# Expert retrieval of an encoder block: V of three token tiles by one stream of the whole table, with one-hot matrices made on VectorE

## The chip, the cores and the metric

The kernel runs on one core of one Trainium2 chip. The metric is the device time of one execution in microseconds (us). The core has five engines that each run their own list of instructions in order and meet only at semaphores: TensorE (PE, matrix products into PSUM), VectorE (DVE), ScalarE (ACT), GpSimd (POOL) and SyncE (SP). Transfers run on 16 DMA engines that all queues share. POOL issues the gathers (queue q0), SP the plain loads and stores (queue q1).

## What is computed

One layer of a hybrid encoder over 1024 tokens of width 1024, in f32: an input projection, a bidirectional state-space branch, neighbourhood attention, an output projection, and then a product-key retrieval of experts ("PEER"). The change touches the retrieval alone:

```python
def chunk(xc):                                   # 128 tokens
    q = (xc @ w_q).reshape(128, 8, 2, 128)
    s = einsum('thzd,znd->thzn', q, sub_keys)    # scores of 128 keys, twice per head
    s1, i1 = top_k(s[:, :, 0], 16);  s2, i2 = top_k(s[:, :, 1], 16)
    cand = s1[..., :, None] + s2[..., None, :]
    top, pos = top_k(cand, 16)                   # 16 of 256 pairs
    eidx = (i1 * 128 + i2) at pos                # one of 16384 experts
    gate = softmax(top)
    act = gelu(einsum('thkd,td->thk', u[eidx], xc))
    return einsum('thk,thkd->td', gate * act, v[eidx])
```

Each token picks 8 x 16 = 128 experts, and needs their rows of two tables, `peer_u` and `peer_v`, each of 16384 rows of 1024 f32 (4 KB a row, 64 MB a table).

## The kernel before, in words

The 1024 tokens are 8 tiles of 128 (`TT`). The front of the kernel (conditioning, input projection, state-space scan) ends some 920 us after the start. What follows is `stage_tail`, laid out by hand on a line of **slots**: slot `n` is pick `n % 128` of tile `n // 128`, 1024 slots in all, and every engine's program is written slot by slot. Work of the other branches (attention, state-space recurrence, projections, in three passes of two tiles) is spread over slots -128 to 756 as "lane" jobs: PE products into three PSUM banks `ps_l`, each evicted by ACT or DVE.

In slot `n` of the retrieval:

- POOL issues one gather from `peer_u`: for each of 128 tokens (partitions) the row of its pick, 128 rows x 4 KB = 512 KB, into one of `RU` = 6 rooms (`u_rows`). It waits until DVE has used the room (`u_used`, six slots back).
- DVE waits for the gather and forms the 128 dot products with one instruction of 128 x 1024 (line 2637).
- POOL also issues one gather from `peer_v`, 45 slots behind (`FETCH_AT` and one grain): here the 128 partitions hold 32 picks of 4 tokens. It goes into one of `RV` = 12 rooms (`v_rows`) and waits until PE has summed that room's last content (`v_used`). POOL issues V of a slot ahead of U of the same slot.
- Every fourth slot PE sums four gathered V rooms into `acc` (line 2683) with the weights that ACT has put into `spread`.

The picks of a tile are worked out on DVE ("route": top-16 searches) ahead of their slots. A *grain* is 32 picks (two heads); a tile has 4. `turn_index` and `turn_weight` transpose a grain's indices and weights on PE through the bank `ps_turn`, so that V can be gathered token by token. At the end of a tile `finish_sum`, `finish_square` and `finish_norm` add the residual and normalise on DVE, and SP stores the tile.

So before the change every slot from 45 on moves two gathers of 512 KB, 2048 in all, and after slot 1023 only the last 45 of V are left.

## Time and profile before

| | us |
|---|---|
| median of 3 runs | 4027.4 (4024.05 to 4028.98) |
| the profiled execution: its span | 4023.9 |
| of it: start to the first dot of slot 0 | 920.8 |
| slots 0 to 127 (stage A) | 363.6 |
| slots 128 to 383 (stage B) | 820.6 |
| slots 384 to 639 (stage C) | 781.9 |
| slots 640 to 767 (stage D) | 402.4 |
| slots 768 to 1023 (stage E) | 664.6 |
| after the last dot (stage F) | 70.0 |

The bounds of the stages are the starts of the dot of slots 0, 128, 384, 640 and 768 and the end of the last. The profile is one execution as the hardware recorded it; its own time is the span. A row of the table of waits names who waited, on which line, for whom, then the total, the number of times and the longest.
### The profile page before, as it was taken

The page shows a single profiled execution, that of the slowest core. Times are in us where ns is not written, and L with a number is a line of the kernel's source. Part 1 is how long each engine was busy: PE and PEld are TensorE (multiplying, and loading weights), DVE is VectorE, ACT ScalarE, POOL GpSimd, SP SyncE. Part 2 cuts the span into 40 slices and gives each one's busy share as a digit, 9 for nine tenths or more (in the row PEclk, how much of TensorE's full clock was granted, in tenths as well). Part 3 has the DMA queues.
Part 4 walks back from the last instruction along what each step waited for, and adds up shares of the span by engine and source line. Part 5 has one row for each costly group of instructions (what it writes and reads, how often), then busy time and mean ns, then how long its engine had stood idle before and what let it go on. Part 6 is the DMA issues. An engine that isn't in the chain of part 4 may idle for free.

```text
span 4023.9 us, 41489 instructions
## 1 busy us (share of the span) xinstructions
PE 2788.8 (69%) x14155; PEld 1429.4 (36%) x14155; DVE 2439.3 (61%) x5186; ACT 858.2 (21%) x2057; POOL 2121.6 (53%) x2149
## 2 busy tenths in 40 slices
PE   6899999898975677796676767455757753333334
PEld 4787777544342322333333323122323320000000
DVE  4552446527676666556766665677766667666652
ACT  4333213402143301112333011132320110000000
POOL 1000205013576656556766565676665667777775
PEclk9999999999987888897887888778888875565566
DMA  8944865567999999999999999999999999999998
GB/s 223 258 154 143 228 209 169 180 240 268 413 407 393 403 410 412 413 412 393 393 400 405 412 400 413 401 406 397 392 406 411 389 409 409 410 408 408 402 409 336
DMA packets 472416, 1422.97 MB, mean 354 GB/s; under 512 B 66152, under 2 KB 136784, under 8 KB 464016
## 3 DMA queue, kind: packets, MB, share of 16 engines
q0 software_dynamic: 298768, 1086.75, 69.5%
q1 hardware_dynamic: 173152, 332.95, 23.2%
q8 instruction: 115, 1.88, 0.2%
q10 hardware_dynamic: 288, 0.62, 0.1%
q14 instruction: 93, 0.76, 0.0%
HBM read 1359.46 MB, written 90.06 MB: 360 GB/s over the span
## 4 chain that ended last, share of the span: by engine, by line
DMA 38%; POOL 13%; PE 9%; issue 8%; DVE 8%; ACT 0%; SPq 0%; DVEq 0%; ACTq 0%; POOLq 0%
DMA ring<-in_peer_u,idx 34%; POOL ring L2459 6%; POOL ring L2452 6%; PE ps_l L1775 5%; DMA ring<-in_peer_v,idxT 4%; DVE ring L2637 4%; PE acc L2683 2%; PE ps_l L1853 1%; PE ps_l L1831 0%; DMA lane<-state_scr 0%; DVE e_f L2560 0%; PE ps_l L1848 0%; DVE hit L2558 0%; DVE where L2520 0%; DVE rest L2521 0%
## 5 line engine op out<-in xcount | busy, mean ns | idle before, releaser
L2637 DVE CUSTOM_DVE_ANT_0 ring<-ring,ps_n2F 128x1024 f32<-128x1024 f32 x1024 | 1242.2, 1220 | 933.3 <-DMA ring<-in_peer_u,idx 922.2
L2459 POOL DMA_INDIRECT ring<-in_peer_u,idx x1024 | 999.1, 976 | 805.8 <-DVE dots L2637 576.3
L2683 PE MATMUL acc<-ring,spread 128*32 128x512 f32 x4096 | 734.7, 853 | 953.3 <-DMA ring<-in_peer_v,idxT 953.1
L2452 POOL DMA_INDIRECT ring<-in_peer_v,idxT x1024 | 993.0, 970 | 336.5 <-issue 297.5
L1775 PE MATMUL ps_l<-lane 128*128 128x512 f32 x1760 | 790.2, 603 | 11.6 <-ACT lane L2100 6.6
L2683 PEld LDWEIGHTS acc<-ring,spread 128*32 128x32 f32 x4096 | 147.7, 136 | 1417.6 <-issue 1415.7
L1775 PEld LDWEIGHTS ps_l<-lane 128*128 128x128 f32 x1760 | 330.8, 193 | 443.8 <-issue 431.4
L562 POOL DMA_DIRECT2D bias<-rpb_scr x16 | 13.2, 829 | 322.5 <-PE ps_dt L846 277.0
L1970 PE MATMUL ps_l<-lane 128*128 128x512 f32 x192 | 117.3, 696 | 56.1 <-DVE nmax L2152 55.8
L2489 ACT ACTIVATE dots<-dots 128x32 f32<-128x32 f32 x32 | 7.3, 229 | 606.1 <-DVE dots L2637 605.9
L2060 ACT ACTIVATE st<-st,nmax 128x512 f32<-128x512 f32 x128 | 92.2, 720 | 184.0 <-DVE nmax L2152 182.9
L846 PE MATMUL ps_x<-n_hi,w_x_hi 128*128 128x512 f32 x256 | 103.9, 406 | 13.1 <-DVE w_x_lo L681 13.1
L846 PE MATMUL ps_x<-n_hi,w_qk_hi 128*128 128x512 f32 x256 | 103.2, 403 | 6.6 <-DVE w_qk_lo L757 6.6
L688 DVE TENSOR_TENSOR w_z_lo<-w_z,w_z_hi 128x512 fp32r<-128x512 f32 x64 | 40.7, 688 | 109.1 <-ACT w_z_hi L588 75.1
L1996 PEld LDWEIGHTS ps_l<-lane 128*64 128x64 f32 (+1 forms) x1664 | 66.2, 146 | 108.0 <-ACT lane L2040 56.5
L846 PE MATMUL ps_x<-n_lo,w_x_hi 128*128 128x512 f32 x256 | 102.3, 399 | 0.0
L846 PE MATMUL ps_x<-n_hi,w_x_lo 128*128 128x512 f32 x256 | 102.1, 399 | 0.0
L846 PE MATMUL ps_x<-n_lo,w_qk_hi 128*128 128x512 f32 x256 | 101.9, 398 | 0.0
L846 PE MATMUL ps_x<-n_hi,w_qk_lo 128*128 128x512 f32 x256 | 101.8, 397 | 0.0
L1996 PE MATMUL ps_l<-lane 128*64 128x64 f32 (+1 forms) x1664 | 84.4, 241 | 23.2 <-ACT lane L2040 22.9
L2018 PE MATMUL ps_l<-ident,st 128*128 128x128 f32 x448 | 73.9, 289 | 31.5 <-ACT lane L2049 31.1
L2266 POOL TENSOR_TENSOR ring<-lane,ring 128x4096 f32<-128x4096 f32 x2 | 17.7, 8832 | 139.7 <-DMA lane<-in_w_out 139.7
(363 smaller groups left out, 4014.7 us busy)
## 6 DMA issues: line engine op xcount, KB each, us to landing
lane<-kept_scr SPq DMA_DIRECT2D x44, 2048.0 KB, 10.6
w_z<-in_w_in SPq DMA_DIRECT2D x16, 1024.0 KB, 6.0
adaB<-in_w_ada SPq DMA_DIRECT2D x16, 1024.0 KB, 6.2
ring<-in_peer_u,idx POOLq DMA_INDIRECT x1024
ring<-in_peer_v,idxT POOLq DMA_INDIRECT x1024, 13.8
kept_scr<-in_w_in SPq DMA_DIRECT2D x6, 2048.0 KB
lane<-w_scr SPq DMA_DIRECT2D x6, 2048.0 KB, 10.9
ada<-in_w_ada SPq DMA_DIRECT2D x8, 1024.0 KB, 15.4
```

The costliest lines, as they stand in the source:

```text
L688: nc.vector.tensor_tensor(z_parts[1][q % PLACES][:, :], w_z[:, k // KH, k % KH, :], z_parts[0][q % PLACES][:, :], ALU.subtract).then_inc(z ...
L846: last = nc.tensor.matmul(bank, stationary(left, k), moving(right, k), start=(k == 0 and n == 0), stop=(k == KD - 1 and n == 2))
L1775: last = nc.tensor.matmul(bank, inT[:, f % SETS, k, :], spare_half(c, k // 4)[:, k % 4, :] if weights is None else weights[:, k, :], start ...
L1853: last = nc.tensor.matmul(ps_y[:, h * HEADDIM:(h + 1) * HEADDIM], M4[:, d, h, :], x_dt[:, i, d, hc], start=False, stop=(d == 1 and h == HP ...
L1970: nc.tensor.matmul(scores_bank(a_pass, u), qd[:, p % RP, i, :], kT[:, p % RP, k0:k0 + HALF], start=True, stop=True).then_inc(qk_done, 1)
L1996: last = nc.tensor.matmul(values_bank(a_pass, u)[side(hh), :], PT[keys, u % 2, b, side(hh)], V[keys, p % RP, tile, side(hh)], start=(j == ...
L2018: last = nc.tensor.transpose(turned[:, b * P:(b + 1) * P], probs[:, u % RS, c0:c0 + P], ident[:, :])
L2060: nc.scalar.activation(row[:, GRID_W:], row[:, GRID_W:], ACT.Exp, bias=least, scale=-1.0, accum_out=rsum[:, u % 4:u % 4 + 1]).then_inc(exp ...
L2452: pool.indirect_dma_start(v_rows[:, nv % RV, :], None, a["peer_v"][0], bass.IndirectOffsetOnAxis(ap=idxT[:, m % 2, col:col + 1], axis=0)). ...
L2459: pool.indirect_dma_start(u_rows[:, n % RU, :], None, a["peer_u"][0], bass.IndirectOffsetOnAxis(ap=idx[:, i % RI, j:j + 1], axis=0)).then_ ...
L2637: nc.vector.tensor_tensor_reduce(out=u_rows[:, n % RU, :], in0=u_rows[:, n % RU, :], in1=ps_n[:, :], scale=1.0, scalar=0.0, op0=ALU.mult, ...
L2683: last = nc.tensor.matmul(acc[q * QUAD:(q + 1) * QUAD, cols], spread[:, m % 2, c0:c0 + QUAD], v_rows[:, nv % RV, cols], start=(g == 0 and ...
```

## The change

V of tiles 2, 3 and 4 (`DENSE`) is no longer gathered. Instead:

- **Weight matrices.** For each of the 384 tokens of these tiles a matrix of 128 x 128 is made, whose entry (b, a) is the sum of the weights of the picks with first key a and second key b. DVE makes two one-hot matrices per token with one `tensor_scalar` each (`both_hot`; the second also multiplies by the weight), PE multiplies them (`make_parts`, 4 tokens in one PSUM bank, `ps_turn`), ACT evicts the bank into `parts`, and after 16 tokens ACT itself issues a store of 1 MB into a new DRAM tensor `share_scr`, in pieces of 512 bytes. The room `parts` is single: before it writes the first four tokens of the next 16, ACT waits for that store (`s_stored`). The four rooms of one-hot matrices are single too: DVE waits for the product that read the room four tokens earlier (`part_mm`). `make_parts` stands every third slot (a slot or two later where `ps_turn` is needed otherwise) from slot 9 of the tile that follows, ACT's eviction one slot later.
- **One stream of the table.** From slot 770 to 1046 the whole table `peer_v` is loaded once, in 32 blocks of 512 rows (2 MB) by SP, and the weight matrices are loaded again (48 loads of 0.5 MB). PE multiplies them for the three tiles at once: 192 units of 4 products of 128 x 512 (`multiply_block`) into the three banks `ps_l`, which the lane jobs have left by then. DVE adds each unit to its sum in SBUF two slots later (`add_block`). The three tiles are normalised and stored at the end (`whole_sum` and what follows it).
- **Pace of the gathers.** V of tiles 0 and 1 is spread out: its 256 gathers are issued over 640 slots (two in five slots) from slot 45. Tiles 5 to 7 keep one a slot, 45 slots behind, from slot 685.
- **Rooms.** V has 10 rooms in place of 12, and only 7 until row 340 of V (slot 769), since the other three hold `parts` and the one-hot matrices until the last store. `h` has a room of its own in the ring, and indices and weights are kept for 4 tiles.

All dot products with U, the routes and the lane jobs stay in their slots.

```diff
+DENSE = (2, 3, 4)
+KEYS_TOGETHER = 4
+SHARES = NKEYS // KEYS_TOGETHER
+PART_KEYS, PART_TOKENS = 8, 16
...
+    share_scr = [scratch(f"share_scr_t{t}", [NKEYS // PART_KEYS, NKEYS, P // PART_TOKENS, PART_KEYS * PART_TOKENS]) for t in DENSE]
...
-    RU, RV, RI = 6, 12, 2
+    RU, RV, RI, RH = 6, 10, 2, 4
+    RING = 18
...
-        v_rows = ring[:, RU * DM:].rearrange("p (r d) -> p r d", d=DM)
+        v_rows = ring[:, RU * DM:(RU + RV) * DM].rearrange("p (r d) -> p r d", d=DM)
+        h = ring[:, (RU + RV) * DM:(RU + RV + 1) * DM]
+        kept_row = ring[:, (RU + RV + 1) * DM:(RU + RV + 2) * DM]
+        parts = v_rows[:, RV - 2:RV, :].rearrange("p r d -> p (r d)")
+        pick_row = v_rows[:, RV - 3, :].rearrange("p (s n) -> p s n", n=P)
+        pickT, hot_a = pick_row[:, 0:3, :], pick_row[:, 4:4 + TURNS, :]
+        hot_b = kept_row[:, RH * PICKS:RH * PICKS + TURNS * P].rearrange("p (s n) -> p s n", n=P)
+        weight = kept_row[:, 0:RH * PICKS].rearrange("p (r n) -> p r n", r=RH)
...
+        order = {t: i for i, t in enumerate(SUMMED)}
+        v_grain = [GRAINS * t + g for t in SUMMED for g in range(GRAINS)]
+        pace = GRAINS * (DENSE[-1] + 1) / (GRAINS * len(BEFORE))
+
+        def fetch_slot(s, k):
+
+            m = v_grain[s]
+            if m < GRAINS * DENSE[0]:
+                return FETCH_AT + int(pace * (s * GRAIN + k))
+            return m * GRAIN + FETCH_AT + k
...
+        ALL_ROWS_FROM = PICKS * len(BEFORE) + 84
+        v_row = [nv % (RV - 3) if nv < ALL_ROWS_FROM else (nv - ALL_ROWS_FROM) % RV for nv in range(len(SUMMED) * PICKS)]
...
+            n += PART_AT - PICK_TURN_AT
+            for k in range(P // TURNS):
+                while turning & {n, n + 1}:
+                    n += 1
+                part_mm_at[n], part_ev_at[n + 1] = i * P // TURNS + k, i * P // TURNS + k
+                for r, before in enumerate((2, 2, 1, 1)):
+                    hot_at.setdefault(n - before, []).append(i * P + k * TURNS + r)
+                n += PART_STEP
...
+        DENSE_FROM, DENSE_TO, DENSE_LAG = PICKS * 6 + 2, PICKS * TT + 22, 2
...
+        unit_slot = [DENSE_FROM + q * (DENSE_TO - DENSE_FROM) // ALL_BLOCK_UNITS for q in range(ALL_BLOCK_UNITS)]
+        unit_at, added_at, block_at = {}, {}, {}
+        for q, n in enumerate(unit_slot):
+            unit_at.setdefault(n, []).append(q)
+            added_at.setdefault(n + DENSE_LAG, []).append(q)
...
+        v_blocks = a["peer_v"][0].rearrange("(c i b) d -> c b i d", i=KEYS_TOGETHER, b=NKEYS)
...
+        def load_shares(sp, c):
+
+            if c == 0:
+                sp.wait_ge(p_mm, LANE_JOBS)
+                sp.wait_ge(p_norm, TT)
+                for r in range(MIX):
+                    sp.wait_ge(s_keep[r], 16 * TT // MIX)
+            if c >= 2:
+                sp.wait_ge(block_mm, (c - 1) * UNITS_A_SHARE)
+            sp.dma_start(v_block[:, c % 2, :, :], v_blocks[c]).then_inc(s_block[c % 2], 16)
+            s, first = divmod(c * KEYS_TOGETHER, PART_KEYS)
+            if first == 0:
+                if s == 0:
+                    sp.wait_ge(s_stored, 16 * ND * P // PART_TOKENS)
+                for i in range(ND):
+                    sp.dma_start(shares[s % 2][i], share_scr[i][s].rearrange("b g n -> b (g n)")).then_inc(s_part[s % 2], 16)
+
...
+                            if v_before[nv] is not None:
+                                pool.wait_ge(v_used, v_before[nv] // QUADS + 1)
+                            elif nv >= ALL_ROWS_FROM:
+                                pool.wait_ge(s_stored, 16 * ND * P // PART_TOKENS)
...
+                        if n in part_ev_at:
+                            k = part_ev_at[n]
+                            group, turn = divmod(k * TURNS, PART_TOKENS)
+                            act.wait_ge(part_mm, (k + 1) * TURNS)
+                            if k and turn == 0:
+                                act.wait_ge(s_stored, 16 * group)
+                            nc.scalar.activation(parts.rearrange("p (c t e) -> p t c e", t=PART_TOKENS, e=PART_KEYS)[:, turn:turn + TURNS, :, :],
+                                                 ps_turn[:, :].rearrange("p (t c e) -> p t c e", t=TURNS, e=PART_KEYS), ACT.Copy).then_inc(part_ev, 1)
+                            if turn == PART_TOKENS - TURNS:
+                                act.wait_ge(part_ev, k + 1)
+                                d, g = divmod(group, P // PART_TOKENS)
+                                nc.scalar.dma_start(share_scr[d][:, :, g, :].rearrange("c b n -> b c n"),
+                                                    parts.rearrange("p (c n) -> p c n", n=PART_KEYS * PART_TOKENS)).then_inc(s_stored, 16)
...
+                def both_hot(u):
+
+                    if u >= TURNS:
+                        v.wait_ge(part_mm, u - TURNS + 1)
+                    k = u % P
+                    nc.vector.tensor_scalar(hot_a[:, u % TURNS, :], every_key[:, :], pickT[:, 0, k:k + 1], None, ALU.is_equal).then_inc(hot_a_done, 1)
+                    nc.vector.tensor_scalar(hot_b[:, u % TURNS, :], every_key[:, :], pickT[:, 1, k:k + 1], pickT[:, 2, k:k + 1], ALU.is_equal, ALU.mult).then_inc(hot_b_done, 1)
...
+                def add_block(q):
+
+                    c, i, half = block_unit(q)
+                    total = whole[i][:, half * HALF:(half + 1) * HALF]
+                    bank = ps_l[:, q % LANE_BANKS * HALF:(q % LANE_BANKS + 1) * HALF]
+                    if q == 0:
+                        v.wait_ge(p_mm, LANE_JOBS)
+                        v.wait_ge(p_act, LANE_ACTS)
+                        for k in range(len(st_jobs))[-RS:]:
+                            stored_wait(v, k)
+                    v.wait_ge(block_mm, q + 1)
+                    if c == 0:
+                        nc.vector.tensor_copy(total, bank).then_inc(block_added, 1)
+                    else:
+                        v.wait_ge(block_added, q - UNITS_A_SHARE + 1)
+                        nc.vector.tensor_tensor(total, total, bank, ALU.add).then_inc(block_added, 1)
...
+                def turned_bank_read(kind, number):
+
+                    if turned_last[0] is not None:
+                        was, i = turned_last[0]
+                        if was == "index":
+                            pe.wait_ge(idxT_done, i + 1)
+                        elif was == "weight":
+                            pe.wait_ge(spread_done, TOGETHER * (i + 1))
+                        elif was == "picks":
+                            pe.wait_ge(picks_split, i + 1)
+                        else:
+                            pe.wait_ge(part_ev, i + 1)
+                    turned_last[0] = kind, number
...
+                def make_parts(k):
+
+                    pe.wait_ge(hot_a_done, (k + 1) * TURNS)
+                    pe.wait_ge(hot_b_done, (k + 1) * TURNS)
+                    turned_bank_read("parts", k)
+                    for r in range(TURNS):
+                        nc.tensor.matmul(ps_turn[:, r * P:(r + 1) * P], hot_b[:, r, :], hot_a[:, r, :], start=True, stop=True).then_inc(part_mm, 1)
...
+                def multiply_block(q):
+
+                    c, i, half = block_unit(q)
+                    bank = ps_l[:, q % LANE_BANKS * HALF:(q % LANE_BANKS + 1) * HALF]
+                    if q == 0:
+                        pe.wait_ge(p_act, LANE_ACTS)
+                        pe.wait_ge(p_dve, LANE_DVES)
+                    if q % UNITS_A_SHARE == 0:
+                        pe.wait_ge(s_block[c % 2], 16 * (c // 2 + 1))
+                        s = c * KEYS_TOGETHER // PART_KEYS
+                        pe.wait_ge(s_part[s % 2], 16 * ND * (s // 2 + 1))
+                    if q >= LANE_BANKS:
+                        pe.wait_ge(block_added, q - LANE_BANKS + 1)
+                    s, first = divmod(c * KEYS_TOGETHER, PART_KEYS)
+                    share = shares[s % 2][i].rearrange("p (n e) -> p e n", e=PART_KEYS)
+                    for k in range(KEYS_TOGETHER):
+                        last = nc.tensor.matmul(bank, share[:, first + k, :], v_block[:, c % 2, k, half * HALF:(half + 1) * HALF],
+                                                start=(k == 0), stop=(k == KEYS_TOGETHER - 1))
+                    last.then_inc(block_mm, 1)
```

## Rows read from the trace of the kernel before

**Rows 1.** The page: span, busy times of the engines, DMA share in 40 slices.

```profile
span 4023.9 us, 41489 instructions
...
PE 2788.8 (69%) x14155; PEld 1429.4 (36%) x14155; DVE 2439.3 (61%) x5186; ACT 858.2 (21%) x2057; POOL 2121.6 (53%) x2149
...
DMA  8944865567999999999999999999999999999998
```

**Rows 2.** Windows of stages A to F: PE, PEld, DVE, ACT, POOL busy (instructions), clock, DMA, GB/s.

```profile
920.80:1284.40 363.60, 285.75 (x1252) 139.76 (x1254) 256.42 (x584) 104.61 (x278) 218.83 (x220) 0.88 0.98 382
1284.40:2105.00 820.60, 601.42 (x3256) 270.87 (x3252) 524.53 (x1216) 201.06 (x541) 506.07 (x514) 0.87 1.02 404
2105.00:2886.90 781.90, 513.34 (x2800) 223.26 (x2792) 519.94 (x1192) 173.02 (x474) 498.34 (x513) 0.81 1.02 404
2886.90:3289.30 402.40, 285.25 (x1483) 120.36 (x1486) 256.28 (x591) 71.70 (x182) 244.75 (x256) 0.84 1.01 402
3289.30:3953.90 664.60, 232.77 (x1148) 50.30 (x1140) 437.85 (x968) 39.32 (x95) 486.37 (x510) 0.56 1.03 408
3953.90:4023.90 70.00, 36.88 (x200) 7.74 (x200) 6.98 (x12) 2.57 (x7) 34.01 (x36) 0.65 0.78 305
```

**Rows 3.** Waits of DVE, the longest of stages A to E in order: us, times, longest.

```profile
DVE ring L2637 <- DMA ring<-in_peer_u,idx: 75.4, 44, 5.2
...
DVE ring L2637 <- DMA ring<-in_peer_u,idx: 260.7, 160, 7.9
...
DVE ring L2637 <- DMA ring<-in_peer_u,idx: 236.6, 155, 6.3
...
DVE ring L2637 <- DMA ring<-in_peer_u,idx: 132.5, 78, 9.0
...
DVE ring L2637 <- DMA ring<-in_peer_u,idx: 217.1, 176, 3.5
```

**Rows 4.** DMA view of stage E: gathers issued, median us to landing.

```profile
ring<-in_peer_v,idxT POOLq DMA_INDIRECT x259, 13.3
ring<-in_peer_u,idx POOLq DMA_INDIRECT x251
```

**Rows 5.** DMA view of 46 to 58 us, stores of 512-byte pieces: packets, MB, share.

```profile
q1 hardware_dynamic: 3988, 2.00, 58.1%
...
n_scr<-BT SPq DMA_DIRECT2D x6, 384.0 KB, 2.8
```

**Rows 6.** Lines 724, 2193 and 2213 on DVE: ns min/median/max, start, form.

```profile
L724 DVE TENSOR_SCALAR conv<-padded,taps x16: 750/754/755, 68.1 to 271.4; 128x1024 f32<-128x1024 f32 x16
...
L2193 DVE TENSOR_SCALAR lstat<-lstat x8: 153/154/155, 874.4 to 3144.7; 128x1 f32<-128x1 f32 x8
...
L2213 DVE TENSOR_TENSOR lane<-lane,ps_l x14: 681/685/689, 884.7 to 3142.7; 128x512 f32<-128x512 f32 x14
```

**Rows 7.** Groups of DVE before 920 us, one row: count, busy us, mean ns.

```profile
L1061 DVE TENSOR_TENSOR cb<-ps_cb,upto 128x128 f32<-128x128 f32 x8 | 2.3, 285 | 0.7 <-PE ps_cb L1123 0.7
```

**Rows 8.** Groups of ACT from 920 us on, one row: busy us, mean ns.

```profile
L2123 ACT ACTIVATE lane<-ps_l 128x512 f32<-128x512 f32 x12 | 7.2, 597 | 45.3 <-PE ps_l L1775 45.3
```

**Rows 9.** DMA view of 1332.3 to 1338.0 us: packets, MB, share, by queue.

```profile
DMA packets 1073, 2.10 MB, mean 368 GB/s; under 512 B 593, under 2 KB 593, under 8 KB 1073
...
q0 software_dynamic: 537, 1.97, 94.0%
q1 hardware_dynamic: 536, 0.13, 11.4%
```

**Rows 10.** Line 2452, gathers of V: us from issue to landing.

```profile
DMA to landing us min/median/max: 7.0/13.8/25.3
```

**Rows 11.** Window of line 1775 alone: PE busy, PEld busy, clock, DMA, GB/s.

```profile
980.55:1018.51 37.96, 37.96 (x88) 16.57 (x88) 1.00 0.85 322
```

**Rows 12.** Window of line 2683 alone, stage E: same columns.

```profile
3289.30:3953.90 664.60, 231.05 (x1020) 43.23 (x1012) 0.56 1.03 408
```

**Rows 13.** Waits of POOL, stage E, one row: us, times, longest.

```profile
POOL ring L2452 <- PE acc L2683: 4.4, 10, 1.7
```

More of the change, by code:

```diff
@@ L1187, in stage_tail @@
     LANE_BANKS = 3
+    TURNS = 4
     ctx = ExitStack()
@@ new lines, in stage_tail @@
+        for c in range(SHARES):
+            block_at.setdefault(unit_slot[(c - 1) * UNITS_A_SHARE] + 1 if c >= 2 else DENSE_FROM - 6 + c, []).append(c)
+        WHOLE_SUM = DENSE_TO + DENSE_LAG + 2
+        RESIDUAL_SLOT, WHOLE_ROOT, WHOLE_NORM = PICKS * (TT - 1) + 8, WHOLE_SUM + 3 * ND + 1, WHOLE_SUM + 3 * ND + 4
+        LANE_JOBS = len(evac_of)
+        LANE_ACTS, LANE_DVES = acts, dves
+        DROOM = KEYS_TOGETHER * DM
+        v_block = lane[:, 0:2 * DROOM].rearrange("p (r a d) -> p r a d", r=2, a=KEYS_TOGETHER)
```

284 lines of the change are left out of this document (191 added, 93 removed).

## The prediction, made before the change was run

> **What bounds the kernel now.** I read the page first, then the windows by stage, then who waits for whom. On the page the DMA digits stand at 9 from slice 11 on, while PE, DVE and POOL are busy 53 to 69% [rows 1]. The windows say the same stage by stage: the DMA share is 0.98 in A and 1.01 to 1.03 in B to E (packets overlap a little, so about 1.02 is full), and no engine fills its stage [rows 2]. The waits of DVE confirm it: its one long wait in each stage is for the gather of U [rows 3]. So from slot 0 on, 3103 of 4024 us, the 16 DMA engines bound the kernel. In E almost nothing but gathers moves: 259 + 251 gathers in 664.6 us [rows 2, 4], so one gather of 512 KB costs **1.30 us** of all DMA engines. That is the price for the rest of this text.
>
> The second limit is DVE. Stage time less its wait for U is the time that DVE needs for everything else [rows 2, 3]: A 288, B 560, C 545, D 270, E 448 us. It will matter once transfers are taken away.
>
> **The change, part by part.** In total it takes away 384 gathers of V (499 us at 1.30) and adds the table (32 loads of 2 MB, as much as 128 gathers: 166 us), the loads of the weight matrices (48 of 0.5 MB: 62 us) and 24 stores of 2048 pieces of 512 bytes. For these the row of the 512-byte stores gives 3988 packets in 58.1% of 12 us, 1.75 ns of all engines each [rows 5], so 3.6 us a store and 86 us in all. On the DMA engines alone the balance is 499 - 166 - 62 - 86 = **185 us** to the good. But it is uneven: what is removed lies in slots 45 to 685, what is added lies in slots 770 to 1046, where DMA is full already. So I go by stages.
>
> A (363.6): V falls from 83 to 33 rooms, -50 x 1.30 = -65, to 299; but V starts at slot 45 and the first half runs behind the last projection jobs of PE, which gain nothing. Middle between 299 and 363.6: **331**.
>
> B (820.6): V falls from 256 to 102, -154 x 1.30 = -200. DMA then needs 620, DVE 560. Neither is even over the stage, so now one and now the other will be last, and I take 4% on top: **645**.
>
> C (781.9): the same -200, and 16 of the 24 stores, +57: DMA needs 639. DVE gets 256 tokens x 2 one-hot instructions of 128 x 128. Their price: `tensor_scalar` took 754 ns for 1024 elements a partition and 154 for one [rows 6], on a straight line 229 for 128; bounds are 154 and the 285 of a two-operand instruction of 128 x 128 [rows 7]. I take 225, nearest to the same kind of instruction: 512 x 0.225 = 115 us (79 to 146). DVE then needs 545 + 115 = 660 (624 to 691) and is the bound. ACT's evictions at about 0.6 us [rows 8], 64 here, go beside an ACT that is busy 173 of 782 [rows 2], and PE's small products beside a PE that gives up three fifths of its V sums; both cost nothing while their queue is not held up.
>
> The waits added here are the open point. ACT waits for the store three slots after it issued it; behind that wait stand gelu, the spreading of weights and the evictions of the lane. PE's next `make_parts` but one needs ACT's eviction, and DVE's one-hot instructions stand behind that product, six slots after the store was issued; at 2.7 us a slot DVE has 16 us in hand. What does a store take? Alone 2.8 us for 768 pieces [rows 5]. Beside gathers, small packets and gather packets go through one for one: in a stretch of 5.7 us there are 537 packets of q0 and 536 of q1, 256 bytes for the most part [rows 9]. 2048 pieces at that pace need 4 x 5.7 + 2.8 = 25.6 us while the gather queue is never empty. With DVE as the bound that queue is empty part of the time (DMA work 639 of 660), and V's rows are few, so the store lands sooner; I allow 2.5 us a store, between 0 and 9.2: 16 x 2.5 = 40. **700**.
>
> The Trainium skill ("DMA: Bandwidth & Descriptors", § Queues, rings and completion order) says that a DMA engine takes turns between its queues by whole packets, typically 9 to 17 descriptors. The trace agrees on turns, but shows them at the grain of single pieces. By the page a store's 128 pieces an engine would be 8 to 14 turns, each against at most one gather's share (8 pieces of 0.165, by 1.30 x 16 / 128): 14 to 22 us a store; the allowance of 40 us would nearly vanish and the sum be about 3952.
>
> D (402.4): V falls from 128 to 45 x 0.4 + 83 = 101, -35; 8 stores +29: DMA needs 396, DVE 270 + 58 = 328. From slot 685 to 769 V goes at one a slot with 7 rooms. Then the last row of a batch of four reuses a room of the batch just ahead, so four slots must hold one trip from issue over landing (7.0 to 25.3, median 13.8 [rows 10]) to the sum: 4 x 3.3 = 13 us against that median. It fits only because POOL's pause thins the queue that makes the landing long; I allow 15 us (0 to 60). **411**.
>
> E (664.6): 92% of the stream lies here, (166 + 62) x 0.92 = +210: DMA needs 875. DVE adds 177 units at 0.685 [rows 6], 448 + 121 = 569, covered. POOL still has its two gathers a slot, 486 busy us [rows 2], covered. PE gets 707 products of 128 x 128 x 512, two records each, at 38.0/88 = 0.431 us a record at full clock [rows 11]: 609 us, beside 231 us of V sums at clock 0.56 [rows 12], 130 at full clock: 739 us of full-clock work in 875. In B a busy PE was granted 0.87 [rows 2]: 849. So PE is nearly as late as DMA. V has 10 rooms, so a room must come back within seven slots, 24 us, against a landing of 13.3 now [rows 4] plus the queue of the stream; POOL waited 4.4 us for V's rooms here so far [rows 13]. I allow 15 us: **890**.
>
> F (70.0): 8% of the stream, +18, and 3 for the closing of three more tiles, which lies ahead of the last sum: **91**.
>
> Sum: 331 + 645 + 700 + 411 + 890 + 91 = 3068 in place of 3103, -35 us. The profiled span of 4024 stands 3.4 us below the median, so the forecast is 4027.4 - 35, about **3992 us**: most of the 185 us of DMA time is given back in C (DVE) and by stages that are no longer evenly filled.
>
> **Rivals.** (1) *The store holds ACT, and ACT holds all* (slower). If the gather queue stays full, each store takes 25.6 us and DVE loses 25.6 - 16.4 = 9.2 us at each of 16 stores in C; in D a slot is 3.3 us, six are 20, so 5.6 us at each of 8. 147 + 45 = 192 in place of 40, about 4140 us. It decides from a landing of some 16 us on. For it speaks the row of packets one for one [rows 9]; against it, that a waiting DVE stops the gathers, which empties the queue and speeds the store. (2) *PE bounds the stream* (slower). If PE, held by every V row in turn, is granted 0.75 rather than 0.87, E takes 739/0.75 = 985, +95: about 4087. It decides below 0.84, where PE passes DMA's 875. For it: clock 0.56 in E now; against it: 0.81 to 0.88 wherever PE had lane work [rows 2]. (3) *All stages run at the larger of their two limits*: A 320, B 625, C 660, D 396, E 875, F 88, together 2964, about 3888. For it: POOL is busy in E for 486 of 665 us beside a full DMA and costs nothing [rows 2]; two near limits need not add up. Against: the room rules above.
>
> **How the numbers follow.** Chances: my forecast (3950 to 4040) 0.42, rival 3 (or most of it) 0.21, rival 1 0.22, rival 2 0.15. Within 0.2% is +-8 us, about what a measurement of this kernel can tell from no change. The forecast case is faster with 0.28, the same with 0.08, slower with 0.06; rival 3 is faster; rivals 1 and 2 are slower but for 0.02. Faster 0.49, same 0.10, slower 0.41. Cases of both signs hold much, so the range goes from 3895 to 4130: it leaves out the better half of rival 3's end and the worse half of rival 1's. The likeliest case's own range is 3950 to 4040.
>
> **What would show it.** In the profile after: DMA work by stage and DVE's wait for U. If B falls by about 175 us, the price per gather is right. If C falls by about 80 with DVE's wait for U near zero, DVE is its bound; if C doesn't fall and DVE waits for PE at the one-hot lines and ACT for the store's landing, it is rival 1. If E is over 940 with PE busy over 90% and DMA share under 0.97, it is rival 2. POOL's wait for PE's V sums in D gives the price of the seven rooms. The prediction is wrong if one-hot instructions take near 0.4 us, or if the stream is not hidden behind PE at all.

## The result, and the profile after

| | before | after | predicted |
|---|---|---|---|
| median | 4028.09 us (4 runs) | 4153.28 us (4 runs, 4150.12 to 4163.51) | 3992 (3895 to 4130) |
| after / before | | 1.0321, 95% interval 1.0307 to 1.0336 | 0.991 |
| A, slots 0 to 127 | 363.6 | 337.5 | 331 |
| B, 128 to 383 | 820.6 | 662.0 | 645 |
| C, 384 to 639 | 781.9 | **788.5** | 700 |
| D, 640 to 767 | 402.4 | **452.0** | 411 |
| E, 768 to 1023 | 664.6 | 888.9 | 890 |
| F, after the last dot | 70.0 | 109.3 | 91 |

The change made the kernel 3.2% slower, and the prediction had the sign wrong. The stages are those of one profiled execution, the slowest of the four (span 4161.3, as a run 4163.5). They add up to 3238 in place of the forecast 3068: 170 us too many, of which C has 88, D 41 and F 18.

The page of after, its span, busy times and DMA share in 40 slices (answers to [rows 1]):

```profile
span 4161.3 us, 43453 instructions
...
PE 3294.9 (79%) x14737; PEld 1971.8 (47%) x14737; DVE 2713.7 (65%) x6146; ACT 894.5 (21%) x2099; POOL 1758.0 (42%) x1766
...
DMA  8945865568999999999887987999899999999996
```

Before, the DMA digits are 9 from slice 11 to the last but one. Now there are holes between slices 20 and 30, which lie in C and D. The windows of stages A to F (columns as in [rows 2]) say how large they are:

```profile
923.10:1260.60 337.50, 259.83 (x1028) 133.76 (x1026) 254.74 (x581) 103.70 (x273) 167.57 (x167) 0.88 0.92 339
1260.60:1922.60 662.00, 521.76 (x2560) 257.46 (x2560) 512.68 (x1204) 193.02 (x519) 355.10 (x359) 0.88 0.98 376
1922.60:2711.10 788.50, 504.97 (x2615) 291.74 (x2616) 617.44 (x1695) 200.58 (x513) 356.45 (x359) 0.79 0.87 314
2711.10:3163.10 452.00, 307.10 (x1622) 154.53 (x1624) 314.05 (x852) 89.01 (x210) 214.68 (x223) 0.83 0.92 349
3163.10:4052.00 888.90, 782.54 (x2564) 473.51 (x2556) 545.89 (x1146) 39.14 (x96) 492.84 (x517) 0.95 1.02 408
4052.00:4161.34 109.34, 84.17 (x320) 43.82 (x320) 32.19 (x44) 2.79 (x8) 36.88 (x38) 0.86 0.64 233
```

C has 0.87 x 788.5 = 686 us of DMA work and 617 us of DVE work, and takes 788: neither fills it. So the reader asks who waits there. The waits of DVE, ACT and PE in C, the longest of each (who waited, for whom, total us, times, longest):

```profile
DVE ring L2746 <- PE ps_turn L2918: 94.1, 19, 21.5
DVE idxT L2802 <- PE ps_turn L2868: 21.0, 2, 20.0
DVE ring L2822 <- DMA ring<-in_peer_u,idx: 12.6, 6, 3.3
...
ACT ring L2612 <- PE ps_turn L2918: 197.2, 46, 11.4
ACT ring L2612 <- DMA share_scr_t<-ring: 191.8, 12, 33.0
...
PE ps_turn L2918 <- DVE ring L2747: 70.9, 13, 8.8
PE ps_turn L2918 <- ACT ring L2612: 60.9, 6, 18.5
PE ps_turn L2868 <- ACT ring L2612: 25.0, 2, 24.2
```

Line 2822 is the dot (2637 before), 2746 and 2747 the one-hot instructions, 2918 the product of weight matrices, 2612 ACT's eviction of it. DVE's wait for U, 236.6 us before [rows 3], is 12.6: DMA no longer bounds C. In its place stands a chain: ACT waits 192 us for stores to land, PE waits 61 and 25 us for ACT, DVE 94 us for PE.

The queue that ACT's stores use and their landing, DMA view of C (packets, MB, share; then issues, KB, median us to landing):

```profile
q10 hardware_dynamic: 33024, 16.78, 7.2%
...
share_scr_t<-ring ACTq DMA_DIRECT2D x16, 1024.0 KB, 18.0
```

7.2% of 788.5 is 57 us of all DMA engines, just what the prediction charged for them. The 18.0 us to landing are the trouble, as the first experiment shows. One store shows how. The timeline of ACT, PE and DVE around it (start, us, engine, line, operation; in brackets the idle time before and what ended it):

```profile
2199.69 0.60 ACT L2612 ACTIVATE ring<-ps_turn 128x512 f32<-128x512 f32 x1 [9.35 <-PE ps_turn L2918]
2200.32 0.37 ACTq L2617 DMA_DIRECT2D share_scr_t<-ring  x1
2217.55 0.60 ACT L2612 ACTIVATE ring<-ps_turn 128x512 f32<-128x512 f32 x1 [17.26 <-DMA share_scr_t<-ring]
2218.04 1.08 ACT L2116 ACTIVATE lane<-ps_l 128x512 f32<-128x512 f32 x2
...
2219.27 3.75 PE L1791 MATMUL ps_l<-lane 128*128 128x512 f32 x4 [9.71 <-ACT lane L2116]
2222.81 1.44 PE L2918 MATMUL ps_turn<-ring 128*128 128x128 f32 x8
...
2213.89 1.22 DVE L2822 CUSTOM_DVE_ANT_0 ring<-ring,ps_n2F 128x1024 f32<-128x1024 f32 x1
2215.03 0.08 DVE L2822 DVE_READ_ACCUMULATOR2_ANT dots<- 128x1 f32 x1
2223.48 0.29 DVE L2746 TENSOR_SCALAR ring<-every_key,ring 128x128 f32<-128x128 f32 x1 [8.37 <-PE ps_turn L2918]
```

The store goes out at 2200.3 and lands 17.1 us later. DVE runs on until 2215.1 and then stands 8.4 us. Of these only 2.4 lie before the landing (in most of the long waits more does, see below): after it ACT evicts the bank, then a lane bank (line 2116), PE makes the lane product that waited for that (3.75 us), and only then the product that DVE waits for.

In D and E the same table has, for POOL and ACT in D, DVE in E, and DVE in F:

```profile
POOL ring L2570 <- PE acc L2900: 126.6, 20, 23.4
...
ACT ring L2612 <- DMA share_scr_t<-ring: 105.0, 6, 26.2
...
DVE ring L2822 <- DMA ring<-in_peer_u,idx: 313.5, 180, 12.1
...
DVE st L2764 <- PE ps_l L2936: 38.3, 9, 7.5
```

### The profile page after: what moved, and what is told of

It reads as the page before. It is cut to its first block and busy times, and to the rows that moved or that the text cites. A ratio compares the mean times of both kernels' runs of the same rounds, so it can differ in the third digit from the quotient of the medians.

```text
span 4161.3 us, 43453 instructions
## 1 busy us (share of the span) xinstructions
PE 3294.9 (79%) x14737; PEld 1971.8 (47%) x14737; DVE 2713.7 (65%) x6146; ACT 894.5 (21%) x2099; POOL 1758.0 (42%) x1766
## 5 line engine op out<-in xcount | busy, mean ns | idle before, releaser
L1791 PE MATMUL ps_l<-lane 128*128 128x512 f32 x1760 | 799.7, 609 | 65.0 <-ACT st L2121 27.2
L2570 POOL DMA_INDIRECT ring<-in_peer_v,idxT x640 | 622.0, 972 | 424.8 <-PE acc L2900 245.8
L2936 PE MATMUL ps_l<-lane 128*128 128x512 f32 x1280 | 583.5, 610 | 6.0 <-DMA lane<-share_scr_t 6.0
L1791 PEld LDWEIGHTS ps_l<-lane 128*128 128x128 f32 x1760 | 334.9, 195 | 488.5 <-issue 449.6
L2900 PE MATMUL acc<-ring,spread 128*32 128x512 f32 x2560 | 380.7, 721 | 232.4 <-DMA ring<-in_peer_v,idxT 232.2
L2936 PEld LDWEIGHTS ps_l<-lane 128*128 128x128 f32 x1280 | 396.4, 315 | 199.5 <-issue 63.1
L2918 PE MATMUL ps_turn<-ring 128*128 128x128 f32 x768 | 134.4, 331 | 174.5 <-DVE ring L2747 70.9
L2918 PEld LDWEIGHTS ps_turn<-ring 128*128 128x128 f32 x768 | 123.3, 238 | 216.8 <-DVE ring L2746 123.0
L2746 DVE TENSOR_SCALAR ring<-every_key,ring 128x128 f32<-128x128 f32 x384 | 112.0, 292 | 114.0 <-PE ps_turn L2918 113.9
L1986 PE MATMUL ps_l<-lane 128*128 128x512 f32 x192 | 128.7, 760 | 45.7 <-DVE columns L2168 45.7
L2747 DVE TENSOR_SCALAR ring<-every_key,ring 128x128 f32<-128x128 f32 x384 | 133.7, 348 | 0.0
L2076 ACT ACTIVATE st<-st,columns 128x512 f32<-128x512 f32 x128 | 92.1, 720 | 147.5 <-DVE columns L2168 146.3
L2764 DVE TENSOR_TENSOR st<-st,ps_l 128x512 f32<-128x512 f32 x124 | 84.7, 684 | 52.5 <-PE ps_l L2936 52.5
L2936 PE MATMUL ps_l<-lane,gin 128*128 128x512 f32 x256 | 116.7, 606 | 0.0
## 6 DMA issues: line engine op xcount, KB each, us to landing
share_scr_t<-ring ACTq DMA_DIRECT2D x24, 1024.0 KB, 18.4
```

The source lines that it names most:

```text
L1791: last = nc.tensor.matmul(bank, inT[:, f % SETS, k, :], spare_half(c, k // 4)[:, k % 4, :] if weights is None else weights[:, k, :], start ...
L1986: nc.tensor.matmul(scores_bank(a_pass, u), qd[:, p % RP, i, :], kT[:, p % RP, k0:k0 + HALF], start=True, stop=True).then_inc(qk_done, 1)
L2076: nc.scalar.activation(row[:, GRID_W:], row[:, GRID_W:], ACT.Exp, bias=least, scale=-1.0, accum_out=rsum[:, u % 4:u % 4 + 1]).then_inc(exp ...
L2570: pool.indirect_dma_start(v_rows[:, v_row[nv], :], None, a["peer_v"][0], bass.IndirectOffsetOnAxis(ap=idxT[:, m % 2, col:col + 1], axis=0) ...
L2746: nc.vector.tensor_scalar(hot_a[:, u % TURNS, :], every_key[:, :], pickT[:, 0, k:k + 1], None, ALU.is_equal).then_inc(hot_a_done, 1)
L2747: nc.vector.tensor_scalar(hot_b[:, u % TURNS, :], every_key[:, :], pickT[:, 1, k:k + 1], pickT[:, 2, k:k + 1], ALU.is_equal, ALU.mult).the ...
```

## The experiments

Line numbers move by a few between these kernels. Stages are given as in the table; in every run A lies between 334 and 342 and B between 652 and 665, so only C to F are told; E ends here, and in the column before, at the start of the last dot and in the column after at its end, 1.2 us later. All runs but two were timed once, with the kernel before at a median of 4021.5 to 4028.4 us beside them. Four executions of the changed kernel lie 13 us apart, and the B of all runs, which these edits hardly touch, 12: a step of 10 us in a stage shows nothing. Theories of the first runs: the store's landing (S) and the price of the one-hot instructions (H).

### Stores in 128 pieces of 8 KB

```diff
...
-nc.scalar.dma_start(share_scr[d][:, :, g, :].rearrange("c b n -> b c n"),
-                    parts.rearrange("p (c n) -> p c n", n=PART_KEYS * PART_TOKENS)).then_inc(s_stored, 16)
+nc.scalar.dma_start(share_scr[d][g], parts).then_inc(s_stored, 16)
```

> The store of 16 tokens goes out as 128 pieces of 8 KB in place of 2048 of 512 bytes (same bytes, other order in DRAM, and the loads of the stream keep their 4 KB pieces, so tiles 2 to 4 get weight matrices in the wrong order). Theory S (ACT's wait for the store holds PE and DVE): the landing falls from a median of 18.4 us to some 8, ACT's wait for it in stage C from 192 us to under 30, C from 788 to about 700 and D from 452 to about 420; the whole about 4035. Rival H (the one-hot instructions are too dear: 282 + 342 ns a token in place of 450) and rival L (DVE, PE and ACT wait for one another at every four tokens, store or not): C falls by at most 25, the whole stays over 4120.

Measured: 4060.8 us (before on the same chip 4023.8); C 712.0, D 429.1, E 880.3, F 109.3. The DMA view of this run over the whole kernel, where the changed kernel has 18.4 in the last column, and ACT's wait for the store in C:

```profile
share_scr_t<-ring ACTq DMA_DIRECT2D x24, 1024.0 KB, 8.1
```

```profile
ACT ring L2612 <- DMA share_scr_t<-ring: 69.8, 8, 12.1
```

The same bytes, in a sixteenth of the pieces, land in 8.1 us instead of 18.4, ACT waits 70 us instead of 192, DVE 34 for the products instead of 94, and C and D give back 76 and 23 us. The whole run is 93 us faster than the changed kernel's median, which is 125 us slower than before.

### One-hot matrices for one token in four

```diff
 if u >= TURNS:
+    if u % TURNS:
+        return
     v.wait_ge(part_mm, u - TURNS + 1)
...
-pe.wait_ge(hot_a_done, (k + 1) * TURNS)
-pe.wait_ge(hot_b_done, (k + 1) * TURNS)
+pe.wait_ge(hot_a_done, TURNS + k)
+pe.wait_ge(hot_b_done, TURNS + k)
```

> DVE makes the two one-hot matrices for one token of four only; the products of the other three read those of the first four tokens (weights of tiles 2 to 4 are wrong). All waits, products, evictions and stores stay. It takes 288 x 0.62 = 179 us of work from DVE, 119 of it in stage C and 60 in D. Theory H: C falls by 100 or more to under 690, D by 40, the whole to about 4010. Theory S: the waits for the store stay and eat most of it: C falls by under 50, the whole stays over 4090.

Measured: 4137.5; C 766.5, D 448.4. DVE's busy time in C falls from 617 to 532 us, the stage by 22. Of the 85 us that DVE is spared, 33 come back as waits at the next one-hot line (127 for 94) and some 30 as waits elsewhere. The waits of ACT and DVE in C:

```profile
ACT ring L2612 <- DMA share_scr_t<-ring: 209.0, 11, 26.2
...
DVE ring L2748 <- PE ps_turn L2920: 127.2, 23, 22.3
```

With the small pieces in place it is the store that sets the pace, and H alone is not the cause.

### No weight matrices at all, with 7 and with 10 rooms

```diff
-sp.dma_start(shares[s % 2][i], share_scr[i][s].rearrange("b g n -> b (g n)")).then_inc(s_part[s % 2], 16)
+sp.dma_start(shares[s % 2][i], a["peer_u"][0, (s * ND + i) * P:(s * ND + i + 1) * P, :]).then_inc(s_part[s % 2], 16)
...
-if n in part_ev_at:
+if False:
...
-    split_picks(split_at[n])
-    both_hot(u)
-    turn_picks(pick_turn_at[n])
-    make_parts(part_mm_at[n])
```

> No weight matrices are made at all (no one-hot matrices, products, evictions, stores); the stream loads rows of the U table in their place, as many bytes in the same pieces. Tiles 2 to 4 come out wrong. Pace of the gathers, rooms and stream stay. It measures what the making of the matrices costs in all: by the sum of the prediction without stores and one-hot work C is 581 by DMA and 545 by DVE, so about 605; D 367 by DMA, about 385 if seven rooms cost little (theory R, seven rooms of V bound D from slot 685 on: D stays over 410). The whole about 3930 to 3960.

and with that

```diff
-ALL_ROWS_FROM = PICKS * len(BEFORE) + 84
+ALL_ROWS_FROM = 0
```

> As the kernel without weight matrices, and all ten rooms of V in use from the first row on. Theory R (seven rooms bound D): D falls by 25 us or more against that kernel and POOL's wait for the V sums in D from some 100 us to under 20. Rival: D moves by under 8 us, the rooms were not what D waited for.

Measured: 3915.9, C 605.2, D 398.2, E 879.0, F 110.8; with ten rooms of V from the start 3891.5, C 604.2, D 384.0, E 873.5. So making and storing the matrices costs 183 us in C and 54 in D, and the seven rooms cost 14 in D, between the two expectations. C is a DMA-bound stage again here, with share 0.99:

```profile
1920.60:2525.80 605.20, 402.36 (x2099) 201.17 (x2100) 500.33 (x1173) 163.81 (x450) 354.92 (x359) 0.82 0.99 382
```

Were the matrices free, the stream would bring 2.7 to 3.3%.

### Both first edits at once

> Store as 128 pieces of 8 KB and one-hot matrices of one token in four only: both edits of the first two runs at once, so the weight matrices are wrong. It asks what is left of stage C (712 us with the whole store, 605 without any weight matrices). Theory W (what is left is the price of 512 one-hot instructions on an engine that is then the bound): three quarters of them are 0.75 x 256 x 0.453 = 87 us, C 625 to 640, D about 400, total 3960 to 3985. Rival L (the chain DVE, PE, ACT and back over the single rooms holds DVE whatever the instructions take): C over 690, D over 420, total 4040 to 4060.

Measured: 4007.8; C 681.6, D 416.9. Between the two ranges that were expected: 30 us for three quarters of the one-hot instructions (87 by their price). DMA share in C is 0.95 here, so the next limit stands close behind.

### Small pieces at the load instead of the store

The store as in the first experiment, and

```diff
-sp.dma_start(shares[s % 2][i], share_scr[i][s].rearrange("b g n -> b (g n)")).then_inc(s_part[s % 2], 16)
+sp.dma_start(shares[s % 2][i].rearrange("p (g n) -> p g n", n=PART_KEYS * PART_TOKENS),
+             share_scr[i][:, :, s * PART_KEYS * PART_TOKENS:(s + 1) * PART_KEYS * PART_TOKENS].rearrange("g b n -> b g n")).then_inc(s_part[s % 2], 16)
```

> The store goes out in 128 pieces of 8 KB and the stream loads the weight matrices in 512-byte pieces instead (48 loads of 1024 pieces): the same result, with the small pieces moved from where ACT waits for them to where SP's queue is two blocks ahead. Theory S (what hurts is that the store's landing is waited for, not that its pieces cost DMA time): C 712 and D 429 as with the whole store; E gains 86 - 62 = 24 us of DMA work and stands at 905 to 915; total 4080 to 4100. Rival D (the small pieces cost the same wherever they stand): the 92 us come back in E, 970 or more, total 4150.

Measured: 4229.3; C 719.1, D 419.5, E 1062.0. C and D are near those of the whole store, but E is 182 us above that run, far over the 24 of theory S; it is over 970, as rival D has it, but the growth is twice the 92 us that rival D has come back. PE's longest wait in E, and the loads of the weight matrices in the DMA view of E (18.1 us to landing in the run with whole stores):

```profile
PE ps_l L2936 <- issue: 269.4, 14, 22.9
```

```profile
lane<-share_scr_t SPq DMA_DIRECT2D x37, 512.0 KB, 32.7
```

PE stands 14 times, about 19 us each, with 16 sets of loads in all: the wait seems to have moved with the pieces. The trace names no releaser for it; the next edit tells, which issues each load one block of the stream earlier:

```diff
...
-s, first = divmod(c * KEYS_TOGETHER, PART_KEYS)
-if first == 0:
+s = 0 if c == 0 else (c + 1) // 2
+if c % 2 == 1 and c + 1 < SHARES or c == 0:
```

> As the run with the small pieces at the load (stage E 1062 us there, PE waiting 14 times some 19 us for weight matrices that took 31.5 us to land), but each load of weight matrices is issued one block of the stream earlier, some 27 us. Theory S (small pieces cost by being waited for, and 24 us of DMA work otherwise): E 900 to 920, total 4070 to 4100. Rival D (pieces of 512 bytes slow everything beside them): E over 980, total over 4150.

Measured: 4068.6; C 713.5, D 423.0, E 904.0. The same loads take a median of 36.5 us to land, PE waits 1.7 us for them, and the 269 us are gone. E is 23.7 us above the whole-store run, the 24 of DMA work that the price of 1.75 ns a piece gives. So small pieces have two prices: a small one on the engines, and a large one for whoever waits for them.

### More slots between a store and the wait for it

```diff
+base = n
 for k in range(P // TURNS):
+    if k % (PART_TOKENS // TURNS) == 0:
+        n = base + k // (PART_TOKENS // TURNS) * 14
...
-    for r, before in enumerate((2, 2, 1, 1)):
+    for r, before in enumerate((1, 1, 0, 0)):
...
-    n += PART_STEP
+    n += 2
```

> The products of 16 tokens stand two slots apart and then a gap follows (14 slots a group as before), so that ACT's next wait for the store comes some 9 slots after its issue in place of 3 and DVE's some 11 in place of 6; everything else as in the changed kernel. Theory S: a store that lands in 18 us (33 at most) is then over before anyone asks: ACT's waits for the store in C fall from 192 us to under 40, C to 705 to 725, D to 425 to 440, total 4055 to 4085. Rival T (the small pieces themselves delay the gathers, and the wait is only where it shows): C stays at 770 to 790, total 4140 to 4155.

Measured: 4142.6; C 746.0, D 472.1. Neither expectation: C gains 42 us, D loses 20. ACT still waits 107 us in C, 6 times:

```profile
ACT ring L2615 <- DMA share_scr_t<-ring: 107.2, 6, 29.0
```

Two of these stores, issued at 2018.3 and 2065.9, kept ACT until 33.0 and 36.5 us later, where the longest landing in the changed kernel was 32.9. A likely reason, which no run here isolates, is that gathers go on while nobody is held, so that a store with its 2048 pieces lands later: 15 gathers were issued in those 33.0 us, and 8 in the 29.0 us that the same store took in the changed kernel. What D loses was not taken apart further.

### The stream ends earlier

```diff
-DENSE_FROM, DENSE_TO, DENSE_LAG = PICKS * 6 + 2, PICKS * TT + 22, 2
+DENSE_FROM, DENSE_TO, DENSE_LAG = PICKS * 6 + 2, PICKS * TT - 4, 2
```

> The stream's units are spread over slots 770 to 1020 instead of 770 to 1046, everything else as in the changed kernel. It asks what sets stage F (109 us). Theory P (PE works off the units of the last 22 slots after the last dot, 15 units of 8 records at 0.43 us, 52 us): F falls to 55 to 70, E grows by 8% of the PE work if PE is its bound (to about 940) or by less than 20 us if DMA is; total 4110 to 4150. Rival Q (F is the chain of sums, normalising and storing the three tiles and not the stream): F stays above 95.

Measured: 4137.5; E 898.8, F 77.2. Windows of E and F, and DVE's longest wait in F:

```profile
3159.30:4058.10 898.80, 829.72 (x2696) 511.12 (x2692) 554.85 (x1159) 39.10 (x95) 491.63 (x514) 0.97 1.02 405
4058.10:4135.28 77.18, 36.42 (x192) 7.47 (x184) 21.87 (x31) 2.79 (x8) 41.48 (x42) 0.65 0.82 313
```

```profile
DVE acc L2781 <- PE acc L2900: 51.3, 1, 51.3
```

P holds, if less than in full (55 to 70 were expected): without the stream's last units PE has 36 us of work in F instead of 84, and F ends with the last sum of V, as before the change (70.0). E pays some 10 of the 32 us.

### A better version, and half the one-hot work on ACT

Whole stores, small pieces at the load, issued early, the stream's earlier end, and

```diff
+base = n
 for k in range(P // TURNS):
+    if k % (PART_TOKENS // TURNS) == 0:
+        n = max(n, base + k // (PART_TOKENS // TURNS) * 14)
...
```

> As the run before it, and each group of 16 tokens begins 14 slots after the last at the soonest (products three slots apart as before), so that ACT's next wait for a store comes some 5 slots after its issue, and the units of the stream end at slot 1020. Theory S with theory P for stage F: a whole store lands in 8 us (14 at most) and is over before ACT asks for it; C falls from 719 to between 655 (DVE's own 617 and its waits for U and lanes) and 685, D to 400 to 420, F to 75 to 80; total 3990 to 4040. Rival L (the chain DVE, PE, ACT over the single rooms sets C without any wait for a store): C stays at 700 to 720, total 4045 to 4080.

Measured: 4050.9, 1.0068 times before (95% interval 1.0051 to 1.0085); C 704.2, D 421.7, E 918.7, F 76.6. ACT waits 19 us for stores in C, in place of 192, and still C is 704: rival L's figure, not S's. This is the fastest kernel found that computes the same outputs; it is still slower than the kernel before.

The same kernel with the first one-hot matrix made on ACT:

```diff
...
+one = hot_a[:, u % TURNS, :]
+nc.scalar.activation(one, every_key[:, :], ACT.Abs, bias=pickT[:, 0, u % P:u % P + 1], scale=-1.0).then_inc(hot_x, 1)
+act.wait_ge(hot_x, u + 1)
+nc.scalar.activation(one, one, ACT.Relu, bias=1.0, scale=-1.0).then_inc(hot_a_done, 1)
...
-nc.vector.tensor_scalar(hot_a[:, u % TURNS, :], every_key[:, :], pickT[:, 0, k:k + 1], None, ALU.is_equal).then_inc(hot_a_done, 1)
```

> As the run before it, and the first of the two one-hot matrices of a token is made on ACT (the absolute value of key minus pick, then one minus that, cut off at zero) in place of DVE: the same result. ACT is busy 201 of 789 us in C. Theory W (DVE's work is what is left in C): DVE loses 256 x 0.197 = 50 us in C, C falls by 25 to 50 and the total by 30 to 60. Rival L: ACT's two instructions in turn, some 0.6 us a token, lie in the chain over the single rooms, and C stays or rises.

Measured: 4061.6, 1.0086 times before (1.0068 to 1.0104); C 704.6, D 431.5. DVE is busy 568 us in C in place of 616, and the stage doesn't move. So what holds C when stores are hardly waited for? The last three runs take the store away.

### Matrices made and never stored

```diff
-if k and turn == 0:
-    act.wait_ge(s_stored, 16 * group)
...
-    nc.scalar.dma_start(share_scr[d][:, :, g, :].rearrange("c b n -> b c n"),
-                        parts.rearrange("p (c n) -> p c n", n=PART_KEYS * PART_TOKENS)).then_inc(s_stored, 16)
+    pass
...
-sp.dma_start(shares[s % 2][i], share_scr[i][s].rearrange("b g n -> b (g n)")).then_inc(s_part[s % 2], 16)
+sp.dma_start(shares[s % 2][i], a["peer_u"][0, (s * ND + i) * P:(s * ND + i + 1) * P, :]).then_inc(s_part[s % 2], 16)
```

> The weight matrices are made and evicted as in the changed kernel, but never stored, and ACT never waits for a store; the stream loads as many bytes of another table in their place, so the output of three tiles is not the reference's. It splits what making the matrices costs in stage C (183 us between 605 us without them and 788) into making and storing. Theory S: the stores carry it: 57 us of DMA work and the waits for their landing; without them DMA has 599 us of work in C and DVE 617, C is 640 to 670 and D 395 to 415, total 3950 to 3990. Rival L (the chain DVE, PE, ACT over the single rooms carries it; the run with half of DVE's work moved to ACT left C at 704): C 690 to 715, D 415 to 430, total 4010 to 4050.

Measured: 4043.8; C 705.1, D 418.6, L's figures: S had taken the stores for everything. The window of C, and DVE's longest wait in it:

```profile
1923.50:2628.60 705.10, 499.64 (x2616) 288.81 (x2616) 616.46 (x1695) 199.93 (x514) 357.74 (x359) 0.81 0.90 328
```

```profile
DVE ring L2740 <- PE ps_turn L2912: 37.5, 14, 5.3
```

The same with one-hot matrices for one token in four:

> As the run without any store, and one-hot matrices for one token in four only (the weight matrices and the outputs of three tiles are not the reference's). It asks which part of making the matrices carries the 100 us of stage C that are left without a store (605 to 705). Theory W (the 512 one-hot instructions, on an engine that is then the bound): DVE's busy time falls by 84 us, C to 620 to 650, U's wait of DVE rises from 18 to over 40 us; total 3930 to 3985. Rival L (products and evictions wait for each other over the single rooms, whatever DVE has to do): C 685 to 705, DVE's wait for the products at the one-hot lines rises by some 60 us.

Measured: 3965.6; C 641.7, D 407.7. 84 us less of DVE's work bring 63: theory W, though DVE's wait for U rises to 27 us only, not over 40. In the run without a store it is DVE that bounds C. The same two views:

```profile
1922.60:2564.30 641.70, 483.00 (x2616) 277.61 (x2616) 532.80 (x1318) 199.50 (x514) 356.48 (x359) 0.85 0.95 360
```

```profile
DVE ring L2742 <- PE ps_turn L2914: 41.1, 14, 6.7
```

And without any store, with the first one-hot matrix on ACT:

> As the run without any store, and the first of the two one-hot matrices is made on ACT by two instructions (the output of three tiles is not the reference's for want of the stores). With whole stores the same edit left C at 704 though DVE lost 48 us of work. Theory M (there the next limits stood right behind DVE's, DMA with the stores at 0.94 among them): without stores C falls from 705 to 660 to 685. Rival A (ACT's two instructions lengthen the chain by as much as DVE is spared): C stays at 695 to 715.

Measured: 4036.1; C 696.6, D 428.5, rival A. DVE's longest waits in C:

```profile
DVE ring L2749 <- PE ps_turn L2920: 55.7, 18, 8.6
DVE st L2169 <- PE ps_l L1987: 25.0, 9, 4.6
```

The pair of instructions on ACT (0.39 and 0.31 us in the run with stores) spares DVE 48 us; but DVE waits 18 us more for the products and 18 us more for a lane product (25.0 for 7.3), and ACT is busy 352 us in place of 200. That ACT's queue holds both back is argued from this, not shown by a run of its own.

With the other runs this makes a ladder for C, each step by one edit:

| C, us | what is in it | step |
|---|---|---|
| 605 | no matrices | |
| 642 | matrices, a quarter of the one-hot work, no store | +37 |
| 705 | all one-hot work | +63 |
| 712 | stores in 8 KB pieces, and their wait | +7 |
| 788 | stores in 512-byte pieces | +76 |

The step of 7 us is not clear of noise, and the sizes hold in this order alone: the same cut of one-hot work brought 63 us without stores, 30 with whole stores and 22 with small pieces.

## Why the prediction was wrong, point by point

**What bounds the kernel before, and A and B: right, a little cheap.** DVE's wait for U gives back the DMA time that was freed (in B 261 us before, 87 after), and B fell by 159 us where 175 were expected. The price of 1.30 us a gather came from E; in B before the change q0's packets take 1.32 us a gather (82.9% of 820.6 us for 514), after it 1.36 (73.7% of 662 us for 359), in C 1.42. On 359 gathers the rise in B is some 13 of the 17 us by which B was missed.

**C: the charged work was right, the waits were not.** The stores' DMA work is 57 us as charged. One-hot instructions start 0.19 and 0.26 us apart in the timeline, 0.45 us a token, and DVE is busy 117 us longer than without them (617 and 500) where 115 were charged. The timeline of DVE:

```profile
2209.80 0.28 DVE L2746 TENSOR_SCALAR ring<-every_key,ring 128x128 f32<-128x128 f32 x1
2209.99 0.34 DVE L2747 TENSOR_SCALAR ring<-every_key,ring 128x128 f32<-128x128 f32 x1
2210.25 0.28 DVE L2746 TENSOR_SCALAR ring<-every_key,ring 128x128 f32<-128x128 f32 x1
```

Two steps failed, about equally, and make up the 88 us by which C was missed. The first is **the 660 us at which DVE was to bound C if no store held it: 705 were measured without any store.** Less its wait for U that is 705 - 18 = 687, and what the floor of 660 lacks is covered by DVE's waits for the products over single rooms (37.5 us), which were costed at nothing. The second is **40 us for the stores' waits, where 83 were lost** (705 to 788). It rested on two readings.

First, on 16.4 us in hand for every store, and on nothing that follows the landing. Six stores of C made DVE stand for over 5 us (issues of line 2617 against DVE's timeline). It came to stand 10.2 to 19.4 us after the issue, 14.9 in the mean, and of its 79 us 54 lie before the landing and 25 behind it. With 16.4 us in hand the same six landings would have cost 45, near the 40 allowed; the rest is 9 us because DVE stood sooner, and the 25. For what is held isn't the product alone: in the store shown PE's queue has a lane product ahead of it that waits for ACT as well, and runs at a granted clock of 0.50, the lower level, after the standstill. That store of 17.1 us, which by the prediction costs 0.7, cost 8.4, 6 of them behind the landing.

Second, on the hope that a waiting DVE stops the gathers and speeds the store. POOL does stop issuing, but the rooms of U and V hold enough issued gathers to go on. While DVE stood in the store issued at 2015.1, from 2025.3 to the landing, POOL issued one gather, and the queues still moved 4.40 MB of gathers, 8.4 of 512 KB (packets, MB, share):

```profile
q0 software_dynamic: 1218, 4.40, 57.1%
...
q10 hardware_dynamic: 1930, 0.98, 17.1%
```

And in the 17.2 us of the store shown:

```profile
q0 software_dynamic: 1634, 5.95, 84.6%
q10 hardware_dynamic: 2064, 1.05, 20.1%
```

That is 0.6 to 0.8 gather packets for each piece of the store, near the one-for-one of [rows 9], from which the prediction had read 25.6 us for a full queue. (Its sum adds 2.8 us to four times 5.7; 2048 pieces at 536 in 5.7 us are 21.8.) Landings went from 5.8 to 32.9 us. The prediction counted the gather queue alone, but all nine landings above 21 us fall together with 2.1 to 4.9 MB that SP's queue (q1) moved in the same time, and of the other fifteen one has as much (2.4 MB, 17.2 us). No run isolates what that adds.

So rival 1 is what happened: its mark (C doesn't fall, DVE waits at the one-hot lines, ACT for the landing) is what the profile shows, and so is its condition, a landing from some 16 us on: the median in C is 18.0, and the six stores took 17.1 us and more. That its 4140 stands 13 us from the 4153 measured is in part luck. It put 192 us on the stores' waits where 117 were lost (83 in C, 33 in D), and the other 45 us of C with what B and F were missed by filled the gap.

The estimate of 14 to 22 us a store, worked out in the prediction from the turns that the Trainium skill ("DMA: Bandwidth & Descriptors", § Queues, rings and completion order) states, has the median of 18.4 in it, but eight of the 24 landings lie above it and eight below. By its turns a store of 128 pieces an engine meets 8 to 14 gathers' shares of 8 pieces; the 5.95 MB of gathers above are 11.3 such shares on every engine, so the trace agrees. Neither these rows nor the equal counts of [rows 9] tell its grain from single pieces, though the prediction read single pieces from the latter. The sum of 3952 that hung on it took such landings to cost nearly nothing: three within it, of 17.1, 18.9 and 21.5 us, made DVE stand 8.4, 5.4 and 21.5 us.

**D: the rooms right, the rest as in C.** Seven rooms cost 14 us (in the kernel without matrices), where 15 were allowed. DMA work is 0.92 x 452 = 416 us, where 396 were expected, and the stores and their waits cost 33 (419 without, 452 with), where the sum for D had nothing for the waits.

**E: right.** 889 for 890, at DMA share 1.02, PE busy 783 at clock 0.95. Rival 2, a PE at 0.75, fell; so did rival 3, two near limits that don't add up: E is near its limit of 875, but C, which it put at 660, stands at 705 even without any store.

**F: wrong engine.** The 21 us added were taken for DMA work and closing; DMA share is 0.64, and PE's units of the last 22 slots set it. Where the stream ends earlier, F is 77.

## What to carry to other kernels

A transfer has a price in engine time and a time to landing, and with many small pieces beside a full gather queue the second is several times the first: 3.6 us of work, 18 us to land here. If an in-order engine waits for the landing, cost the wait from the landing's upper end, take the slack of the shortest case and not the mean (10 us of 10 to 19 here), and add what stands in the queues behind the one that is released (25 of 79 us here). Either make the pieces large on the side that is waited for, or issue the transfer well ahead: the loads, one block earlier, took 36.5 us to land and held PE for 1.7 us.

## What the runs showed of the hardware

- Two DVE instructions on 128 x 128 overlap in the records: 0.28 and 0.34 us long, they start 0.19 and 0.26 apart. The records' mean is no price in a row of them; their starts are.
- More slack doesn't buy its own length: nine slots in place of three left 107 of 192 us of ACT's waits, and two stores took 33.0 and 36.5 us until ACT went on.
- TensorE's granted clock shows in the tail of a wait: in the 9.7 us from the store on, with PE busy for 3.75, it was 0.50, the lower of the two levels. PE then stood for 9.7 us, and the lane product behind the wait, at 0.50 again, took 3.75 us for four records, where 0.431 a record was read at full clock [rows 11]. The windows:

```profile
2200.30:2210.00 9.70, 3.75 (x16) 3.38 (x16) 9.56 (x26) 0.00 (x0) 5.78 (x6) 0.50 1.06 401
2219.27:2223.02 3.75, 3.75 (x5) 1.68 (x6) 0.00 (x0) 0.00 (x0) 0.00 (x0) 0.50 0.42 168
```
